# Two heads of a pair at once in the array: scores from its row halves without padding, values alternating between its column halves

## What is computed

```python
def retention(q, k, v):                      # 6 heads, decay instead of a softmax
    scores = jnp.einsum('bhcd,bhed->bhce', qc, kc) * decay[None]
    inner = jnp.einsum('bhce,bhev->bhcv', scores, vc)
...
def moba_attention(q, k, v, rel_bias):       # 256 tokens: one own block, causal
    s_own = jnp.einsum('bhqd,bhld->bhql', qi, k_own) * scale + b_own[None]
    s_own = jnp.where(dist_own >= 0, s_own, -jnp.inf)
    p = jax.nn.softmax(logits, axis=-1)
...
# first block: softmax attention with a sink term per head,
# ATT_HEADS = 8, ATT_KV_HEADS = 2, ATT_HEAD_DIM = 64
```

## Time and profile before

| | us |
|---|---|
| runs of the kernel before | 2521.57, 2524.56, 2525.34 |
| median | 2524.56 |
| profiled execution, span from first to last instruction | 2522.7 |
| TensorE busy | 2460.3 |
| VectorE busy | 1816.5 |
| ScalarE busy | 1312.4 |

### The profile page before, as it was taken

How to read it: one execution, slowest core, us unless ns; L and a number is a source line. 1 busy time by engine, 2 the same in 40 slices (tenths; PEclk the granted TensorE clock), 3 DMA queues, 4 the chain that set the end, 5 groups by cost and what they waited for, 6 DMA issues and landing times.

```text
span 2522.7 us, 33560 instructions
## 1 busy us (share of the span) xinstructions
PE 2460.3 (98%) x13301; PEld 1992.0 (79%) x13301; DVE 1816.5 (72%) x2875; ACT 1312.4 (52%) x1992; POOL 66.4 (3%) x71
## 2 busy tenths in 40 slices
PE   7999999999999988999999999999999999999998
PEld 2565648788786767888888888888798999989998
DVE  6788627676432454999999999999777775676774
ACT  3135513222232453877778777777645554545553
POOL 0000010000010000000000000000000000000000
PEclk9999999999999999999999999999899999999999
DMA  7522023555412102989889889898743445433442
GB/s 291 224 99 92 1 84 150 197 201 185 149 67 84 51 17 102 354 334 364 332 332 364 336 334 364 332 367 333 266 168 118 151 181 198 157 134 133 168 184 101
DMA packets 71653, 510.71 MB, mean 202 GB/s; under 512 B 7905, under 2 KB 9057, under 8 KB 10049
## 3 DMA queue, kind: packets, MB, share of 16 engines
q1 hardware_dynamic: 68690, 500.21, 52.1%
q10 hardware_dynamic: 2208, 6.32, 0.7%
q0 software_dynamic: 592, 1.97, 0.2%
HBM read 506.23 MB, written 2.23 MB: 202 GB/s over the span
## 4 chain that ended last, share of the span: by engine, by line
PE 86%; DVE 8%; ACT 4%; issue 1%; DMA 1%; POOL 0%; ACTq 0%; DVEq 0%
PE bank L816 84%; DVE UL L2087 2%; ACT UH L1604 1%; DVE arena L2095 1%; PE bank L1188 1%; DMA consts<-in_c 1%; ACT arena L1607 1%; DVE XT L2095 1%; PE bank L931 1%; ACT XT L1607 0%; DVE arena L2787 0%; DVE HT L2087 0%; DVE arena L2091 0%; DVE small L2154 0%; ACT arena L1831 0%
## 5 line engine op out<-in xcount | busy, mean ns | idle before, releaser
L2087 DVE TENSOR_TENSOR UL<-ring,UH 128x1024 fp32r<-128x1024 f32 (+1 forms) x804 | 970.0, 1218 | 320.8 <-ACT UH L1604 301.0
L1604 ACT CAST UH<-ring 128x1024 fp32r<-128x1024 f32 (+1 forms) x804 | 830.3, 1040 | 560.7 <-PE bank L816 531.2
L816 PE MATMUL bank<-XH,UH 128*128 128x256 f32 x1040 | 302.2, 291 | 4.5 <-DVE UL L2087 3.4
L816 PE MATMUL bank<-XL,UH 128*128 128x256 f32 x1040 | 294.0, 283 | 0.0
L816 PE MATMUL bank<-XH,UL 128*128 128x256 f32 x1040 | 293.9, 283 | 0.0
L816 PE MATMUL bank<-UH,HGh 128*128 128x512 f32 (+1 forms) x768 | 290.5, 378 | 3.4 <-issue 2.3
L816 PE MATMUL bank<-UH,HGl 128*128 128x512 f32 (+1 forms) x768 | 287.4, 374 | 0.0
L816 PE MATMUL bank<-UL,HGh 128*128 128x512 f32 (+1 forms) x768 | 286.7, 373 | 0.0
L2134 DVE CUSTOM_DVE_ANT_0 JUNK<-ring,CROW 128x1024 bf16<-128x1024 f32 x176 | 206.3, 1218 | 13.1 <-ACT CROW L1607 9.9
L816 PE MATMUL bank<-arena 128*64 128x256 f32 (+7 forms) x856 | 197.5, 372 | 13.8 <-ACT arena L1604 4.6
L816 PEld LDWEIGHTS bank<-XH,UH 128*128 128x128 f32 x1040 | 198.8, 191 | 14.4 <-issue 6.7
(11 more groups left out here) (217 smaller groups left out, 4017.0 us busy)
## 6 DMA issues: line engine op xcount, KB each, us to landing
ring<-in_w SPq DMA_DIRECT2D x477, 1024.0 KB, 4.9
XT<-in_x ACTq DMA_DIRECT2D x2, 1024.0 KB, 11.4
bias_scratch<-BIAS POOLq DMA_DIRECT2D x6, 192.0 KB, 2.1
consts<-in_c ACTq DMA_DIRECT2D x1, 1109.0 KB, 7.9
out_y<-XT ACTq DMA_DIRECT2D x2, 512.0 KB, 3.5
BIAS<-bias_scratch POOLq DMA_DIRECT2D x1, 768.0 KB, 7.1
constd<-in_c ACTq DMA_DIRECT2D x1, 768.0 KB, 4.3
consts<-in_c ACTq DMA_DIRECT2D x1, 512.0 KB, 17.0
```

What stands on the lines that cost most here:

```text
L816: return e.matmul(out, lhsT, rhs, start=start, stop=stop, skip_group_check=True)
L1604: return e.copy(out, in_)
L2087: return e.tensor_tensor(out, a, b, op)
```

## The change

Four things change, all in the order and the operands of TensorE's products and in the buffers that they read:

1. `tiles1` and `tiles2` list the two heads of a pair next to each other for one query block, then the same two for the next query block.
2. The scores of both heads of a pair are issued in the even step, into two banks, each as a product of 64 rows: head `2 hp` from rows 0 to 63 of `Q` and `KZ` (or `MQ` and `MK`), head `2 hp + 1` from rows 64 to 127. The zero halves are no longer read. The masks for both follow.
3. The values of both heads are multiplied in one place for one query block (128 moving columns, not 256), and alternate between the two column halves, piece by piece. `PT1` and `PT2` hold four tiles of 128 columns instead of two of 256.
4. `ret_out` alternates between its two heads.

```diff
         def tiles1(l):
-            pairs = ([(h, 0) for h in range(8)] if l == 0 else []) + [(h, 1) for h in range(8)]
-            return [(h, c, qb) for h, c in pairs for qb in range(2)]
-
-        tiles2 = [(h, qb) for h in range(6) for qb in range(2)]
+            return [(2 * hp + r, c, qb) for c in range(l, 2) for hp in range(4) for qb in range(2) for r in range(2)]
+
+        tiles2 = [(2 * hp + r, qb) for hp in range(3) for qb in range(2) for r in range(2)]
...
-                if i < n_t:
+                if i < n_t and i % 2 == 0:
                     h, c, qb = tiles[i]
                     nk = 512 if c else 256
-                    b = take(w, ("sc", l, i))
+                    bs = [take(w, ("sc", l, i + r)) for r in range(2)]
...
-                    op = mm(b[:, 0:nk], Q[:, h // 2, q0:q0 + 128], KZ[:, j, 0:nk], True, not c)
+                    for r in range(2):
+                        part = slice(64 * r, 64 * r + 64)
+                        op = mm(bs[r][:, 0:nk], Q[part, h // 2, q0:q0 + 128], KZ[part, 2 * (h // 4) + r, 0:nk], True, not c)
+                        if not c:
+                            op.then_inc(*sums.up(("sc", l, i + r)))
                     if c:
                         lo = 384 if qb == 0 else 256
                         w.wait_ge(*vec.at("masks"))
-                        op = mm(b[:, lo:lo + 128], IB, WM0 if qb == 0 else WM1, False, True)
-                    op.then_inc(*sums.up(("sc", l, i)))
-                    give(("sc", l, i))
+                        for r in range(2):
+                            mm(bs[r][:, lo:lo + 128], IB, WM0 if qb == 0 else WM1, False, True).then_inc(
+                                *sums.up(("sc", l, i + r)))
+                    give(("sc", l, i), ("sc", l, i + 1))
...
-                    if qb == 0:
+                    if h % 2 == 0:
                         return
...
                     for kb in range(nkb):
-                        op = mm(b[r:r + 64, 0:256], V_A[:, kb, 64 * (h // 4):64 * (h // 4) + 64],
-                                PT1[:, (j // 2) % 2, kb, :], kb == 0, kb == nkb - 1)
-                    op.then_inc(*sums.up(("values", l, j), *([tile] if h % 2 else [])))
+                        for r in range(2):
+                            op = mm(b[64 * r:64 * r + 64, q], V_A[:, kb, 64 * (h // 4):64 * (h // 4) + 64],
+                                    PT1[:, (j - 1 + r) % 4, kb, :], kb == 0, kb == nkb - 1)
+                    op.then_inc(*sums.up(("values", l, j), *([tile] if qb else [])))
...
-                    mm(b[:, 0:nk], MQ[:, h // 2, 128 * qb:128 * qb + 128], MK[:, h, 0:nk], True,
-                       True).then_inc(*sums.up(("sc2", l, i)))
-                    give(("sc2", l, i))
+                    for r in range(2):
+                        part = slice(64 * r, 64 * r + 64)
+                        mm(bs[r][:, 0:nk], MQ[part, h // 2, 128 * qb:128 * qb + 128], MK[part, h + r, 0:nk], True,
+                           True).then_inc(*sums.up(("sc2", l, i + r)))
+                    give(("sc2", l, i), ("sc2", l, i + 1))
...
-                    for kb, lo in ((0, 0), (1, 128)):
-                        op = mm(psum(tile)[r:r + 64, lo:256], MV[:, kb, 64 * h:64 * h + 64],
-                                PT2[:, (j // 2) % 2, kb, lo:256], kb == 0, kb == 1)
+                    for kb in range(qb + 1):
+                        for r in range(2):
+                            g = h - 1 + r
+                            op = mm(psum(tile)[64 * r:64 * r + 64, q], MV[:, kb, 64 * g:64 * g + 64],
+                                    PT2[:, (j - 1 + r) % 4, kb, :], kb == 0, kb == qb)
...
-                    for h in (2 * hp, 2 * hp + 1):
-                        r = 64 * (h % 2)
-                        for s in range(2):
-                            lo = 128 * s
+                    for s in range(2):
+                        lo = 128 * s
+                        for h in (2 * hp, 2 * hp + 1):
+                            r = 64 * (h % 2)
...
-                    copy(PT1[:, (j // 2) % 2, 0:nkb, 128 * qb:128 * qb + 128],
+                    copy(PT1[:, j % 4, 0:nkb, :],
```

More of the change, by code:

```diff
@@ L655, in build @@
         PB1 = view(arena, 18288, 4, 512)
-        PT1 = view(arena, 20336, 2, 4, 256)
+        PT1 = view(arena, 20336, 4, 4, 128)
         AT = view(arena, 22384, 4, 512)
@@ L708, in build @@
         PB2 = view(arena2, 9736, 3, 256)
-        PT2 = view(arena2, 10504, 2, 2, 256)
+        PT2 = view(arena2, 10504, 4, 2, 128)
         SWR2 = view(arena2, 11528, 6, 2, 256)
@@ L904, in attend @@
                 n_t = len(tiles)
-                if i < n_t:
+                if i < n_t and i % 2 == 0:
                     h, c, qb = tiles[i]
                     nk = 512 if c else 256
-                    b = take(w, ("sc", l, i))
+                    bs = [take(w, ("sc", l, i + r)) for r in range(2)]
                     q0 = 256 * c + 128 * qb
-                    j = 2 * (h // 4) + h % 2
                     if c:
@@ L936, in attend @@
                     h, c, qb = tiles[j]
-                    if qb == 0:
+                    if h % 2 == 0:
                         return
                     nkb = 4 if c else 2
-                    r = 64 * (h % 2)
                     tile = ("av", l, c, h // 2)
-                    if h % 2 == 0:
+                    if qb == 0:
                         take(w, tile)
@@ L946, in attend @@
                     w.wait_ge(*act.at("va", l, 3))
+                    q = slice(128 * qb, 128 * qb + 128)
                     for kb in range(nkb):
-                        op = mm(b[r:r + 64, 0:256], V_A[:, kb, 64 * (h // 4):64 * (h // 4) + 64],
-                                PT1[:, (j // 2) % 2, kb, :], kb == 0, kb == nkb - 1)
-                    op.then_inc(*sums.up(("values", l, j), *([tile] if h % 2 else [])))
-                    if h % 2:
+                        for r in range(2):
+                            op = mm(b[64 * r:64 * r + 64, q], V_A[:, kb, 64 * (h // 4):64 * (h // 4) + 64],
+                                    PT1[:, (j - 1 + r) % 4, kb, :], kb == 0, kb == nkb - 1)
+                    op.then_inc(*sums.up(("values", l, j), *([tile] if qb else [])))
+                    if qb:
                         give(tile)
@@ L1253, in attend2 @@
             def attend2(l, i):
-                if i < 12:
+                if i < 12 and i % 2 == 0:
                     h, qb = tiles2[i]
                     nk = 128 * (qb + 1)
-                    b = take(w, ("sc2", l, i))
+                    bs = [take(w, ("sc2", l, i + r)) for r in range(2)]
                     w.wait_ge(*vec.at("mk", l, h // 2))
                     w.wait_ge(*vec.at("mq", l, h // 2))
-                    mm(b[:, 0:nk], MQ[:, h // 2, 128 * qb:128 * qb + 128], MK[:, h, 0:nk], True,
-                       True).then_inc(*sums.up(("sc2", l, i)))
-                    give(("sc2", l, i))
+                    for r in range(2):
[3 more added lines that the diff above has]
+                    give(("sc2", l, i), ("sc2", l, i + 1))
                 if 3 <= i < 15:
@@ L1282, in attend2 @@
                     w.wait_ge(*vec.at("mval", l))
-                    for kb, lo in ((0, 0), (1, 128)):
-                        op = mm(psum(tile)[r:r + 64, lo:256], MV[:, kb, 64 * h:64 * h + 64],
-                                PT2[:, (j // 2) % 2, kb, lo:256], kb == 0, kb == 1)
-                    op.then_inc(*sums.up(("values2", l, j), *([tile] if h % 2 else [])))
-                    if h % 2:
+                    q = slice(128 * qb, 128 * qb + 128)
+                    for kb in range(qb + 1):
[3 more added lines that the diff above has]
+                                    PT2[:, (j - 1 + r) % 4, kb, :], kb == 0, kb == qb)
+                    op.then_inc(*sums.up(("values2", l, j), *([tile] if qb else [])))
+                    if qb:
                         give(tile)
@@ L1821, in attend2 @@
                         w.wait_ge(*sums.at("values2", l, 2 * (j // 2 - 2) + 1))
-                    evict(tile, PT2[:, (j // 2) % 2, 0:qb + 1, 128 * qb:128 * qb + 128],
+                    evict(tile, PT2[:, j % 4, 0:qb + 1, :],
                           psum(tile)[:, 0:128 * (qb + 1)].rearrange("p (k q) -> p k q", q=128))
```

## The result

| | runs | median us | range |
|---|---|---|---|
| before | 7 | 2521.57 | 2517.26 to 2525.34 |
| changed | 7 | 2533.26 | 2526.30 to 2535.51 |

The ratio is 1.0043, with a 95% interval of 1.0031 to 1.0055. The forecast was 2504.3 with a range of 2490 to 2520, so both the sign and the range missed. It was worked out from 2524.56, the median of the first three of the seven runs before; against 2521.57 the change cost 11.7 us. The profiled execution took 2533.49 us, its span is 2531.4.

What follows compares the result with a forecast made beforehand. TensorE was taken to bound the kernel (98% busy), VectorE next in layer 0 only. Of 28.9 us saved, 1.5 + 7.5 + 5.3 + 4.0 + 2.0 = 20.3 arrive: 2524.6 - 20.3 = 2504.3 us, range 2490 to 2520.

Steps and rivals of the forecast that it cites:

- How TensorE's time was costed: All attention: scores save 7.9 us and values 21.0 of TensorE's own time, 28.9 together; retention 0.
- without overlap: Rival, score pairs: row halves don't overlap, so visits lose 13.2 us against 21.0 of values; 2519.4, chance 0.11.
- with program order: Rival, score pairs: a pair takes three record times instead of two, 10.6 us more; 2511, chance 0.07.
- A visit to the row halves: Score pairs: a visit and return cost 0.35 us over its own records, 0.40 in block 2.
- Layer 0: Block 1: 1.5 of 4.6 us arrive beside the projections, 7.5 of 10.4 in the tail; two-step period 4.79 to about 4.
- nine places: Layer 0: places where a tile gets the bank of a score still awaiting its maximum and exponential, 1.59 us each bare.
- Slower: the banks: Rival, layer 0: transposes await the previous score's exponential, 25.4 us over 16 pairs against 20.3 won; 2529.7, chance 0.07.
- steps of 128 and 256 keys change places: Block 2: the new order of these steps was put at 0 us.
- The clock: Rival, shorter tails: two more stretches of some 2.5 us at the lower clock give back 5 us; 2509, chance 0.07.
- layer 1, ahead of the tail: Block 1: VectorE is free for 60% of layer 1, so 5.3 of 5.7 us arrive.
- layer 1, tail: Block 1: three value blocks behind the 3.0 us wait save 3.4 us, with 0.6 ahead of it: 4.0 of 5.3.
- block 2: VectorE has 24 us free of 90 but also makes weight parts TensorE streams: 2.0 of 3.0 us arrive.

Runs made afterwards that it cites:

- padded_pairs_table: bank_table with the two scores of a pair as padded products over the whole array, one after the other; 2517.9 us, ratio 0.9977.
- bank_table: Changed kernel, each take in the attention parts given the free bank read first in its own trace (121 places); 2508.4 us, ratio 0.9947.
- table_layer0: Changed kernel with the table of bank_table in block 1's layer 0 attention alone (45 places); 2531.8 us, ratio 1.0039.
- table_block2: Changed kernel with the table of bank_table in block 2's attention alone (50 places); 2515.8 us, ratio 0.9977.

## Why the prediction was wrong, by its own steps

**How TensorE's time was costed: right.** The tail of layer 0 in the changed kernel:

```profile
221.15 1.09 PE L815 MATMUL bank<-arena 128*64 128x128 f32 x16
222.18 0.66 PE L934 MATMUL bank<-consts,arena 128*128 128x128 f32 x4
222.76 1.13 PE L815 MATMUL bank<-arena 64*128 64x512 f32 x4
223.83 0.29 PE L815 MATMUL bank<-constb 128*128 128x128 bf16 x2
223.95 0.61 PE L934 MATMUL bank<-consts,arena 128*128 128x128 f32 x4
225.54 1.09 PE L815 MATMUL bank<-arena 128*64 128x128 f32 x16 [0.98 <-ACT arena L1612]
227.52 0.65 PE L934 MATMUL bank<-consts,arena 128*128 128x128 f32 x4 [0.88 <-ACT arena L1683]
228.10 1.13 PE L815 MATMUL bank<-arena 64*128 64x512 f32 x4
229.16 0.28 PE L815 MATMUL bank<-constb 128*128 128x128 bf16 x2
```

Two scores of 512 keys take 1.07 us to their masks, where one took 0.86, and 1.19 to the transposes ("about 1.2"). Sixteen records of values take 1.03 ("about 1.0"). The first records of the two products of a pair start 0.007 us apart in the trace. Retention still takes 0.80 us. The rivals without overlap (0.11) and with program order (0.07) are out: row halves do work at once, and padded_pairs_table puts 9.5 us on it. The Trainium skill, "TensorE: Matmul & The Clock Gate", Part 3, "The mechanism", has products start and end in program order, and the trace does not agree: a pair of four records takes 1.07 us, and the second product's first record starts with the first product's first, not behind its second. A visit to the row halves costs 0.20 us over its records, and 0.14 ahead of them where transposes stand before it (222.18 to 222.76, for 0.44): 0.34, against 0.35. In block 2 it is less than the 0.40 on record: a pair of 128 columns, 0.22 us of records, takes 0.42 from 1880.67 to the transpose at 1881.09, and 0.09 ahead of it.

**Layer 0: nearly right.** Its period of two steps was to fall from 4.79 to about 4. It is 5.33 (223.83 to 229.16), of which 1.86 are two stops for ScalarE. With good banks the stretch beside the projections gives 1.6 us (1.5 forecast) and the tail 6.0 (7.5). One of the nine places that were counted did stop TensorE for over 1 us, the values of step 10, again behind a convolution on VectorE:

```profile
155.00 0.76 PE L815 MATMUL bank<-arena 128*64 128x128 f32 x8 [2.79 <-ACT arena L1683]
```

The kernel before stood for 2.54 us at 161.0, for a copy, and that stop is gone. In bank_table the stop at the values is gone and a wait for a copy is back, 3.44 us at 160.16, so the place cost next to nothing. Even with the plain queue VectorE's last maximum came 9.4 us earlier by the traces; 3.6 of them were lost behind it, with the clock at 0.83 in this stretch, against 0.96.

**The step that failed: the banks, and where they were looked for.** The prediction knew that scores issued in pairs change who gets whose bank. It counted places of this kind in layer 0 alone, because VectorE is nearly full there, and priced them at 1.59 us, one maximum, one small step, one exponential. Both are wrong in the same way. A stop for a bank lasts as long as VectorE takes to come to the score, not as long as the score's own steps; and VectorE is furthest behind not where it is busiest on average but where something long stands in front of the score in its program. In layer 1, where it is free for 60% of the time, that is a convolution; in block 2 retention and a weight part. There a place costs 1.2 to 4.7 us. Two in layer 1 and four in block 2 make 16 us of stops, and in layer 0, with its nine places, table_layer0 found 1.5 us. The rival "Slower: the banks" had the right mechanism and the right sign, with a chance of 0.07 and in the wrong layer. That its 2529.7 lies near 2533.3 is luck: it set 25.4 us of stops in layer 0 against the gain, and gave 5.1 us slower where 11.7 came. For block 2 the prediction had said that steps of 128 and 256 keys change places at no cost; their banks were not followed at all.

**The clock: a rival that was too small.** It had two stretches of 2.5 us at most, in the tails. Layer 1 alone lost some 5 us to it ahead of the tail. The lower level came behind a stop of 4.67 us in a stretch that had not stopped in the kernel before.

**What arrives, with the banks settled.**

| stretch | forecast | changed | with table |
|---|---|---|---|
| layer 0, beside projections | -1.5 | -2.2 | -1.6 |
| layer 0, tail | -7.5 | -2.9 | -6.0 |
| layer 1, ahead of the tail | -5.3 | +5.7 | -2.2 |
| layer 1, tail | -4.0 | -2.6 | -2.3 |
| block 2 | -2.0 | +10.9 | -2.4 |
| sum | -20.3 | +8.9 | -14.5 |

The medians say -14.0 for the last column. The term that is still too large is layer 1 ahead of its tail. TensorE's work fell there as it should: 97.0 busy became 93.1, of which 1.7 are a stretch of 3.4 us at the lower clock, so 5.6 us of work went. But 1.9 us came back as idle time, 1.6 of it the one wait for the bank of score 5, and 1.7 through the clock behind that wait. In the tail of layer 1 the wait of 3.0 us for the scans became 4.3: what TensorE saved ahead of it only made it wait longer, and the forecast had counted 0.6 us of that.

**What stays open.** That a stop brings the lower clock is read from their order in the traces (a stop, then the stretch), not from an experiment that keeps TensorE busy through it. Whether pairing the scores costs a few microseconds by itself, and whether it pays as a whole, the runs do not tell from the spread. And the split of the 25 us among the three parts is known only to some 3 us each.

## What to carry to other kernels

When a change makes an engine take a shared buffer earlier or two at a time, follow the queue of buffers through the whole program and put beside each take the time at which the former holder is read in the trace; the places that matter are where the reader has something long in front of it, however idle it is on average. If the order of buffers is a plain queue, test the change once with each take given the buffer that is read first: here that turned 11 us lost into 14 won, with no product or softmax step altered. And make the same edit to the kernel before as a control, since a rule for buffers can cost as much as it saves.

## What the runs showed that was not expected

Two FP32 products in the two row halves of the array ran fully side by side: 1.07 us for both to the mask, against 1.06 for one alone and 1.72 for two padded ones. A stop of TensorE of 4.67 us was followed by 10.2 us at the lower clock, worth about its own length again; shorter ones were followed by less (3.79 us by 6.8, 3.78 by 3.4, and 1.61 in bank_table by 3.4). And the spread of the runs of one kernel, 4 to 16 us and once 20 (table_block2, 2509.9 to 2529.8), is as large as most of the effects here, so that a single profile placed a loss but did not size it. Part of it is the clock in code that no run changed: near 1805 the lower level lasts 13.7 us in the traces of before, changed and table_block2 and 3.4 in that of bank_table.
